# Four instead of eight gate parts ahead of the first attention score, and eleven instead of twelve selection rounds in front, in a two-layer hybrid decoder kernel

## The reference, cut to what matters

```python
D_MODEL, SEQ, DEPTH = 1024, 512, 2          # A_HEADS = B_HEADS = 8, top_k = min(256, SEQ // 4) = 128
def hybrid_layer(x, p_i, ...):
    h = x @ w_in
    qa, ka, va, qi, ki, wi, cq, ckv, kr, conv_in, gate_pre = jnp.split(h, IN_SPLITS, axis=-1)
    ...                                      # rotary embedding, low-rank up projections
    y_a = dsa_attention(qa, ka, va, qi, ki, wi)   # per query: the 128 best keys by an indexer score
    y_b = causal_attention(q_full, k_full, v_b)   # dense causal softmax, 8 heads
    y_c = conformer_conv(conv_in, ...)            # GLU, causal depthwise conv of width 31, LN, swish
    gates = jax.nn.sigmoid(gate_pre.reshape(B, S, N_BRANCH, D_MODEL) + b_gate)
    merged = (gates[:, :, 0] * (y_a @ w_branch[0]) + gates[:, :, 1] * (y_b @ w_branch[1])
              + gates[:, :, 2] * (y_c @ w_branch[2]))
    x = layer_norm(ALPHA * x + merged @ w_out, ln1_g, ln1_b)
    f_gate, f_up = jnp.split(x @ w_ffn_in, 2, axis=-1)
    ffn = (jax.nn.silu(f_gate) * f_up) @ w_ffn_out
    ple = jax.nn.sigmoid(x @ w_ple_gate) * (p_i @ w_ple_proj)
    return layer_norm(ALPHA * x + ffn + ple, ln2_g, ln2_b)
```

## Time and profile before

| | us |
|---|---|
| median of 3 runs | 1768.98 (1768.29 to 1770.74) |
| profiled execution | 1768.52 |
| its span, first to last instruction | 1766.7 |
| TensorE busy | 1743.0 (99%) |
| VectorE, ScalarE, GpSimd busy | 1273.8, 969.3, 886.7 |
| PE waits, whole span: for DVE `sb_pt_l` (6 times) | 2.6 |
| PE waits, whole span: for ACT `sb_pbuf` (2 times) | 1.1 |

### The profile page before, as it was taken

How to read it: one execution, slowest core, us unless ns; L and a number is a source line. 1 busy time by engine, 2 the same in 40 slices (tenths; PEclk the granted TensorE clock), 3 DMA queues, 4 the chain that set the end, 5 groups by cost and what they waited for, 6 DMA issues and landing times.

```text
span 1766.7 us, 29274 instructions
## 1 busy us (share of the span) xinstructions
PE 1743.0 (99%) x10142; PEld 1533.0 (87%) x10142; DVE 1273.8 (72%) x2459; ACT 969.3 (55%) x1909; POOL 886.7 (50%) x518
## 2 busy tenths in 40 slices
PE   9999999999999999999999999999999999999997
PEld 9878888888789999988898788888887899999886
DVE  6279789877799888713363887897868998886033
ACT  4545887843465555622244558877445665655222
POOL 5446679554433343454434565895544343344542
PEclk9999999999999999999999999999999999999999
DMA  5324221223333333233323333222332323322331
GB/s 182 98 94 127 75 75 60 72 84 97 97 118 107 110 96 120 73 123 104 97 89 95 105 108 88 68 60 72 95 98 94 120 97 114 103 99 95 118 103 64
DMA packets 50411, 171.93 MB, mean 97 GB/s; under 512 B 6240, under 2 KB 6496, under 8 KB 50272
## 3 DMA queue, kind: packets, MB, share of 16 engines
q1 hardware_dynamic: 49408, 168.84, 30.3%
q10 hardware_dynamic: 864, 1.28, 0.2%
HBM read 162.76 MB, written 2.10 MB: 93 GB/s over the span
## 4 chain that ended last, share of the span: by engine, by line
PE 91%; DVE 5%; ACT 2%; issue 2%; POOL 0%; DVEq 0%; ACTq 0%; POOLq 0%
PE banks L1234 25%; PE banks L1236 24%; PE banks L1235 24%; PE banks L1291 3%; PE banks L1293 3%; PE banks L1292 3%; PE banks L1403 2%; PE banks L1359 2%; DVE sb_xl L1936 1%; DVE banks L1795 1%; DVE sb_u L1929 1%; DVE sb_u L1899 1%; PE banks L1383 1%; PE banks L1323 1%; PE banks L1384 1%
## 5 line engine op out<-in xcount | busy, mean ns | idle before, releaser
L669 POOL TENSOR_TENSOR sb_wl<-sb_wraw,sb_wh 128x1024 fp32r<-128x1024 f32 x205 | 498.0, 2433 | 509.5 <-ACT sb_wh L813 483.9
L1234 PE MATMUL banks<-sb_xh,sb_wh 128*128 128x512 f32 (+1 forms) x1152 | 403.8, 351 | 1.9 <-ACT sb_h_qa L993 0.8
L1236 PE MATMUL banks<-sb_xh,sb_wl 128*128 128x512 f32 (+1 forms) x1152 | 389.1, 338 | 0.0
L1235 PE MATMUL banks<-sb_xl,sb_wh 128*128 128x512 f32 (+1 forms) x1152 | 388.5, 337 | 0.0
L813 ACT ACTIVATE sb_wh<-sb_wraw 128x1024 fp32r<-128x1024 f32 x199 | 210.3, 1057 | 259.6 <-PE banks L1236 151.3
L1236 PEld LDWEIGHTS banks<-sb_xh,sb_wl 128*128 128x128 f32 x1152 | 218.7, 190 | 24.3
L1234 PEld LDWEIGHTS banks<-sb_xh,sb_wh 128*128 128x128 f32 x1152 | 219.2, 190 | 23.4 <-issue 3.7
L1235 PEld LDWEIGHTS banks<-sb_xl,sb_wh 128*128 128x128 f32 x1152 | 219.6, 191 | 14.1
L1234 PE MATMUL banks<-sb_t_hi,sb_wh 128*128 128x256 f32 x768 | 217.5, 283 | 3.4 <-DVE banks L2207 3.4
L1235 PE MATMUL banks<-sb_t_lo,sb_wh 128*128 128x256 f32 x768 | 217.3, 283 | 0.0
L1236 PE MATMUL banks<-sb_t_hi,sb_wl 128*128 128x256 f32 x768 | 217.3, 283 | 0.0
(11 more groups left out here) (353 smaller groups left out, 4085.9 us busy)
## 6 DMA issues: line engine op xcount, KB each, us to landing
sb_wraw<-in_weights SPq DMA_DIRECT2D x256, 512.0 KB, 3.5
sb_wraw2a<-in_weights SPq DMA_DIRECT2D x24, 512.0 KB, 3.6
sb_wraw2b<-in_weights SPq DMA_DIRECT2D x24, 512.0 KB, 4.4
sb_u<-in_x SPq DMA_DIRECT2D x8, 256.0 KB, 6.5
sb_q_raw<-sb_qn_t SPq DMA_DIRECT2D x16, 128.0 KB, 2.2
sb_k_raw<-sb_kn_t SPq DMA_DIRECT2D x16, 128.0 KB, 2.3
out<-sb_u SPq DMA_DIRECT2D x8, 256.0 KB, 2.1
sb_q_raw<-sb_qr_t SPq DMA_DIRECT2D x16, 64.0 KB, 2.0
```

Source lines behind the costliest of these rows:

```text
L669: nc.gpsimd.tensor_tensor(wl[:, t % WS, :], wraw[:, t % 2, :], wh[:, t % WS, :].bitcast(F32), ALU.subtract).then_inc(lo_ready, 1)
L1234: nc.tensor.matmul(out, wh_, xh_, start=start, stop=False, skip_group_check=onto)
L1235: nc.tensor.matmul(out, wh_, xl_, start=False, stop=False, skip_group_check=onto)
L1236: return nc.tensor.matmul(out, wl_, xh_, start=False, stop=stop, skip_group_check=onto)
```

## The change

The diff has two edits: four gate parts stand ahead of slot 0 instead of eight, and 11 selection rounds instead of 12.

```diff
-SELECT_ROUNDS, SELECT_FRONT = TOPK // 8, 12
+SELECT_ROUNDS, SELECT_FRONT = TOPK // 8, 11
 SELECT = [(k, part, qt) for k in range(SELECT_ROUNDS) for part in range(2) for qt in range(NT - 1, 0, -1)]
 SELECT_LATE = SELECT[6 * SELECT_FRONT:]
 LATE_SLOT = 2
@@
     parts = [(t, k) for t in range(GATES) for k in range(DK)]
     held = 4
-    steps = [("part", p) for p in parts[:DK]]
-    left = parts[DK:len(parts) - held]
+    front = 4
+    steps = [("part", p) for p in parts[:front]]
+    left = parts[front:len(parts) - held]
```

## The result

| | before | after |
|---|---|---|
| median of 4 runs each, us | 1769.46 (1768.29 to 1770.74) | 1777.02 (1776.67 to 1779.75) |
| span of the profiled execution, us | 1766.7 | 1774.9 |

The ratio is 1.0046, 95% interval 1.0034 to 1.0058: the change costs 0.46%, about 8 us. The sign of the sum was right, its size less than half.

What follows compares the result with a forecast made beforehand. The prediction took TensorE, busy 99% of the span, as the bound; terms summed to +1.6 us a layer, +3.2 in both, so 1771.7 profiled and 1772.2 as median of the runs, range 1768.0 to 1777.0.

Steps and rivals of the forecast that it cites:

- slot 10: Tanh and high part leave ScalarE's row in slot 8, so the late turn's gap goes: -1.04 us a layer.
- score 12: Head 3's low parts on GpSimd come late after tile 7's moved high part; TensorE newly waits: +1.3 us a layer.
- the sign that it gave for being wrong: No gap at score 12 or slot 34, or gaps at value products that had none.
- slot 38: No term; the prediction went only through GpSimd's hand-overs to slots, and named no gap at this value product.
- start: Before score 0, four parts fewer and one selection round less keep TensorE and VectorE in step: 0 us.
- score 24: Head 6's low parts on GpSimd lose about all their lead as tile 11's high part moves: +0.2 us a layer.
- slot 34: Tile 13's later high part delays GpSimd's bias, VectorE's mask and low part, then the value product: +1.5 us a layer.
- slots 46, 54, 58: VectorE's denser taps: slot 46's 0.26 us gap stays, slot 58's 0.88 us gap shrinks: -0.35 us a layer.
- The taps: VectorE's third taps in slots 43 and 50: the first leaves slot 46's gap, the second makes VectorE 0.33 us later.
- The slower rival: VectorE becomes the bound; two more sparse heads show a gap, +2.1 us a layer on top, 1776.4 us; chance 0.20.
- Slot 58's -0.35: VectorE 0.33 us later by slot 50's third tap, TensorE one part (0.68 us) more: the 0.88 gap shrinks by 0.35.

Runs made afterwards that it cites:

- e5: The kernel before with only the gate parts changed (four ahead of score 0), twelve selection rounds in front as before: 1780.37 us, ratio 1.0064.
- e10: e9 with ScalarE's two copies of the sparse keys and values in slot 19 instead of slot 8: 1765.70 us, ratio 0.9977.
- e1: The changed kernel with heads 3's and 6's low parts ahead of those of gate tiles 7 and 11 in GpSimd's list: 1776.14 us, ratio 1.0037.
- e11: The changed kernel with only the two copies of the sparse keys and values moved from slot 8 to slot 19: 1774.82 us, ratio 1.0039.
- e2: The changed kernel with the keep bias ahead of two taps and tile 14's low part in GpSimd's list: 1774.50 us, ratio 1.0036.
- e6: The kernel before with only the selection changed (eleven rounds in front), all eight gate parts ahead of score 0: 1770.85 us, ratio 1.0005.
- e12: The changed kernel with six instead of four gate parts ahead of score 0: 1774.33 us, ratio 1.0027.
- e8: e7 with three more taps moved from VectorE to GpSimd (22 of 31 instead of 19): 1766.78 us, ratio 0.9987.
- e3: The changed kernel with both edits of GpSimd's list, those of e1 and e2: 1771.96 us, ratio 1.0014.
- e7: e3 with head 4's three transfers one gate tile earlier in SyncE's list: 1770.46 us, ratio 1.0001.
- e9: The kernel before with only three more taps on GpSimd (22 of 31 instead of 19): 1766.54 us, ratio 0.9988.
- e4: The kernel before with the two edits of GpSimd's list from e3, as a control: 1771.19 us, ratio 1.0012.

## Why the prediction was wrong

Each new wait and the gain stand where the prediction put them, and each sign it listed came: no gap in slot 10, score 12 behind line 714 with 4.86 us from the start of tile 7's low part, VectorE 3.22 us at the bias, gaps at slots 34 and 58 inside the given sizes. But so did the sign that it gave for being wrong, a gap at a value product that had none: slot 38. The sum was +1.6 us a layer and is +3.88. By its terms:

| term, us a layer | predicted (bounds) | measured | tested by |
|---|---|---|---|
| start | 0 (-0.3 to 0.3) | 0.0 | e5: 1.9 to 2.4 without the round |
| slot 10 | -1.04 (-1.04 to 0) | -1.20 | e10 |
| score 12 | +1.3 (0.5 to 1.8) | +1.90, then 0.11 | e1, e11 |
| score 24 | +0.2 (0 to 0.9) | +0.34 | e1, e5 |
| slot 34 | +1.5 (1.2 to 1.8) | +1.87, with 0.08 ahead | e2, e5 |
| slot 38 | not priced | +0.58 | e5, e6, e12 |
| slots 46, 54, 58 | -0.35 (-1.3 to 1.4) | +0.24 + 0.31 - 0.35 = +0.20 | e5, e6, e8 |

The 2.27 us a layer that the sum missed are 0.71 at score 12, 0.58 at slot 38, 0.55 at slots 46 and 54, 0.45 at slot 34 and 0.14 at score 24, less 0.16 at slot 10.

- **Score 12 was mis-sized**, mostly by ScalarE's row. I put the end of the high part at "189.75 at the earliest" and added 0.8 us for the copies of slot 8; it ended at 191.28, which is 190.83 without the 0.45 us by which the whole execution was late. 0.3 us come from there, 0.16 from slot 10, whose larger gain brings TensorE to score 12 sooner, and 0.14 are the hand-over from GpSimd (196.22 to 196.36), which the step left out. e11 shows that the copies of slot 8 were worth the added 0.8: take them away and 0.82 us of wait go. Slot 10's larger gain lies outside its own bound: I had counted 0.16 us more for each of its two gaps than is shown, and the matmuls that followed on the two late ones lost another 0.06 and 0.10 us.
- **Slot 34 was mis-sized** by 0.37 us, 0.07 beyond its bound. I took 2.8 us for the move of tile 13's high part against the slots. GpSimd starts that tile's low part 3.34 us later than before (246.61 against 243.27) and score 33 starts 0.33 later, so it moved 3.0 us: 0.2 more. Another 0.06 is the hand-over to TensorE (265.27 + 0.68 = 265.95 to 266.01). The last 0.1 I didn't take apart.
- **Slot 38 is the step that failed in kind.** The prediction went through every hand-over from GpSimd to a slot, and said so: "each hand-over from GpSimd to a slot loses lead. I go through them." A high part that moves also moves inside ScalarE's own list, and that had no term. Where it falls ahead of copies that VectorE and TensorE wait for, it cost 0.58 us (slot 38; 0.57 in e5 by the gate parts alone, nothing in e6 without them) and 1.06 us (slot 46 in e12). I had asked exactly this of slot 43, and not of slot 36.
- **The taps were put at nothing where they cost**: the third taps of slots 43 and 50 show at slots 46 and 54 (0.15 and 0.29 us in e6, without the gate parts), where I had counted nothing. The slower rival took its condition from that: two more sparse heads with a gap. Slot 38 came with a gap, though for another reason, and slot 54 as 0.3 us of delay with hardly any idle time shown; that is 0.6 and 0.3 us instead of 1.04 each, and VectorE did not become the bound.
- **Slot 58's -0.35 was luck.** I had the third tap of slot 50 make VectorE 0.33 us later, against 0.68 us of one gate part more. But the tap that reads GpSimd's sum ends 0.56 us after GpSimd's low part of tile 26 in the kernel before, in the changed one and in e6, however late it starts inside it, so a third tap has no say there: e6 has one in slot 50 and another in slot 56 and loses 0.08 us. What moved is that low part itself: it starts 1.59 us after score 57 instead of 1.25 (e6: 1.33). These 0.34 us happen to be the size of the 0.33.
- **A chain that was hidden.** Behind score 12's wait stood a second one at slot 14, of 1.3 to 1.9 us (e1, e3); 0.9 us of it in layer 0 and 1.3 in layer 1 were SyncE's queue, 0.6 ScalarE's row (e7). It cost nothing in the changed kernel. A sum of waits can't be turned round: taking one of 1.9 us away gave 0.6 us in layer 0 and 0.2 in layer 1.

The gain that the change could have had was slot 10's 1.20 us a layer. e10 has 0.84 of it by moving two copies, without moving anything that others wait for.

## What to carry to other kernels

When work is dealt out differently over slots, list for every engine what changes places inside its own row, not only what it hands to the others: a 1 us operation that fell ahead of copies on the path cost 0.6 and 1.06 us here, with ScalarE busy only 80% of that stretch. When a gap is traced to a backlog, move the piece of the backlog that nobody wants yet (here two copies wanted 18 slots later) instead of the stream that everything is tied to. And before counting on the removal of a wait, read which queue is next at that place, the transfers' queue among them.

## What the runs showed of the hardware

**The tap and GpSimd's low part: who comes first is not held up.** The tap that reads GpSimd's sum from SBUF met GpSimd's low part in four ways, both with two operands in SBUF. In the earlier trace rows it started 0.17 us after it and took 2.80 us; in the changed kernel it started 0.64 us after it and took 2.33, ending 0.56 us after GpSimd; in e9 it started after GpSimd's end and took 0.76; and in e5 it started 0.15 us before it. There the tap took 0.75 us and GpSimd's operation 2.86 instead of 2.41 (changed kernel, VectorE and GpSimd; then e5):

```profile
334.44 2.33 DVE L1789 SCALAR_TENSOR_TENSOR banks<-sb_hconv,sb_par,sb_praw 128x512 f32<-128x512 f32 x1
```

```profile
333.80 2.41 POOL L670 TENSOR_TENSOR sb_wl<-sb_wraw,sb_wh 128x1024 fp32r<-128x1024 f32 x1 [5.60 <-ACT sb_wh L814]
```

```profile
334.19 0.75 DVE L1789 SCALAR_TENSOR_TENSOR banks<-sb_hconv,sb_par,sb_praw 128x512 f32<-128x512 f32 x1
```

```profile
334.34 2.86 POOL L670 TENSOR_TENSOR sb_wl<-sb_wraw,sb_wh 128x1024 fp32r<-128x1024 f32 x1 [5.75 <-ACT sb_wh L814]
```

This is what the Trainium skill (SBUF — State Buffer, section "SBUF: two separate sides") says of two such operations: the one that starts first has the shared port for its whole instruction. All four cases agree with it in their order; in size the later one loses a little less than that, as shown: the tap ends 0.56 us after GpSimd though it takes 0.75 alone, and GpSimd loses 0.45 us in e5, where the tap runs on for 0.60 us after its start. With the tap ahead (e5) or behind (e9) slot 58's gap is gone, 1.17 and 1.15 us a layer, in e5 with the number of taps unchanged. So the largest gain of any run without the change is one instruction that comes 3 us later.

**Short spells of lower clock.** Seven of the 14 profiled executions hold one or two spells of a few us, ahead of the end of the span, in which the granted clock is below 1.00 (e1, e2, e4, e5, e7, e10, e12); the others, the two kernels among them, hold none. 1.00 is the level of 2.4 GHz; windows of 1 us inside a spell show 0.50, the level of 1.2 GHz, and windows of 4 us with 0.57 to 0.93 hold a part of it. Windows of e2 (span, PE busy, clock, DMA share, GB/s), where one falls right behind the 1.77 us wait of score 12:

```profile
190.00:196.00 6.00, 4.27 (x23) 1.00 0.18 40
196.00:200.00 4.00, 3.96 (x16) 0.70 0.51 157
200.00:204.00 4.00, 4.00 (x21) 0.87 0.00 0
```

It cost 1.6 us in the table of starts (score 15 at +2.35 instead of +0.78). The others stand behind score 12 in layer 1 (e5), at 525 to 528 us (e4, e5, e12) and at about 1400 us (e1, e7, e10). Each of the eight begins 0.4 to 1.6 us after the end of a TensorE wait of 1.76 to 1.87 us. But thirteen other waits of that length have no spell behind them (two of 1.83 and 1.87 us in e6, two of 1.76 and 1.77 us in the changed kernel), so what decides between the two isn't seen here.

Part of the time of e2 and e5 goes with them. Their runs are 1.7 and 3.2 us longer on the mean than the table says, at a mean clock lower by 0.0012 and 0.0020. A spell that costs 1.6 us takes about 0.0009 off the mean clock of 1775 us, so this is about one more spell a run in e2 and two in e5 (an estimate from these numbers). Why those two kernels have more of them is open.
